# Prompt attention of a hybrid encoder layer: heads taken in pairs, values as the stationary operand, the division by the row sums on GpSimd

## The chip, the cores and the metric

One Trainium2 chip, one of its NeuronCores. The kernel is one program with a queue for each engine: TensorE (matmul and transposes; the profile shows its weight loads apart, as PEld), VectorE (DVE), ScalarE (ACT), GpSimd (POOL) and SyncE (SP, which here only issues DMA transfers). Engines wait for each other on counting semaphores. The metric is the device time of one execution in microseconds.

## The reference, cut to what matters

One layer of an encoder over two groups of rows: a prompt of 1024 tokens and 8 sample sequences of 16. Each layer is a token mixer (latent attention with 8 heads, next to a short gated convolution), a cross attention over 256 memory tokens, and a mixture of 32 experts; a layer norm follows each. The change lies in the prompt group's latent attention:

```python
q = (cq @ w_uq).reshape(B, S, 8, 64 + 32)            # 32 of them rotated (rope)
kn, v = split((lat @ w_ukv).reshape(B, S, 8, 64 + 64))
s = (qn . kn + qr . kr) * (96 ** -0.5)               # kr is shared by the heads
s = where(key_chunk <= query_chunk, s, -inf)         # chunks of 64 tokens
attn = softmax(s) @ v                                # (B, S, 8 * 64)
out = concatenate([attn, y_conv], -1) @ w_out        # 1024 x 1024
```

All data are float32. Products that need full accuracy at the faster rate are made of a rounded high part and the rest, in three products: high x high, high x low, low x high.

## The kernel before

The work runs in stages on the same engines: memory keys and values, the input projection of nine row tiles of 128, then the prompt attention (303 to 472 us from the span's start), the sample group's attention, the output product with its layer norm, cross attention, the experts (over a third of the span), and the last norm.

**The loop over steps.** The attention has 64 steps g, head by head (h = g // 8), each with one tile of 128 queries, in the order 2, 4, 6, 7, 5, 3, 1, 0. Tile i sees (i + 1) x 128 keys. Each engine's queue is written out by hand:

- TensorE: `transposes` (L731) turns the probabilities of step g, up to 8 blocks, into PSUM M0. `scores` (L874) for step g + 2 go into T0 or T1 by turns: three products for each 512 keys. `weigh_values` (L892) for step g - 1 has the turned probabilities of a key block as the stationary operand and 64 value columns as the moving one, in plain float32, each product recorded twice. Between them, in steps 4 to 6, stand `keys` (L868) and `turn_queries` (L861) for the next head.
- VectorE: the copy of the turned probabilities from M0 to SBUF (`prT`, two buffers), the reciprocal of the row sum, `row_max` (L1959) for step g + 2, `scale_rows` (L1964), which multiplies the weighed values of step g - 1 by the reciprocal, and the low parts of keys and queries.
- ScalarE: exp with the row sum as its second output (L1554, `pr`, two buffers), the high parts of keys and queries.
- GpSimd: nothing in the loop.

```python
for g in range(PT * H):
    ...
    transposes(M[0], pr[n % 2], ORDER[n] + 1).then_inc(pT_ps, 1)
    ...
    scores(g + 2)
    ...
    weigh_values(g - 1)
```

Keys and queries of a head lie in one of two sets in SBUF (`kT_hi`, `kT_lo`, `qT_hi`, `qT_lo`). Rows 64 to 95 of the keys are the shared rope part and 8 further rows are the mask; they are filled once for each set, by ScalarE, VectorE and GpSimd.

**Before the loop** TensorE makes the values of all heads in T0, T1, M0 and M1, ScalarE copies them out (L1529), and the first head's keys and queries are made. SP issues in order: two constants, the head loads 1 and 2 from DRAM (`load_head`, L524), the eight parts of `w_out`, the sample group's queries, its cache (2 MB), then a head load each time a buffer is free.

**The output product** takes the attention rows (`attn`, query rows in the partitions) and the convolution rows of a tile, turns both with 8 transposes (`turn_mix`, L1026), splits them (ScalarE L1601, VectorE L1845) and runs 48 products of 512 columns (`three_products`, L1014). GpSimd makes the convolution.

## Time and profile before

| | |
|---|---|
| median of 3 executions | 1645.26 us (1645.1 to 1647.88) |
| the profiled execution: time, span | 1648.83 us, 1647.0 us |
| TensorE busy, its mean granted clock | 1571.5 us (95%), 0.98 |
| VectorE, ScalarE, GpSimd busy | 1018.3, 783.7 and 261.3 us |
| bytes moved, mean rate | 351.72 MB, 214 GB/s |

The span is the time between the first and the last recorded instruction. The time of the execution has 1.83 us around it. Matmul records overlap: each lasts some 0.27 us even where the next starts 0.11 us later, so the time of a run of like matmuls is read from its length less the last record's overhang, not from the mean of one record.

### The profile page before, as it was taken

What the parts mean: (1) busy time and instruction counts of PE and PEld (TensorE: products, weight loads), DVE (VectorE), ACT (ScalarE), POOL (GpSimd) and SP (SyncE); (2) the same over time, 40 slices, a digit from 0 to 9 for tenths busy, and PEclk for the clock granted to TensorE, in tenths of its full rate; (3) what the DMA queues carried; (4) which work ended last, traced back from release to release, by engine and by line L of the source; (5) the groups of instructions that cost most, each with busy time, mean ns of one, the idle gap of its engine ahead of it and who ended that gap; (6) DMA issues with size and microseconds to landing.
All of it is one profiled execution on the core that took longest, in us unless ns stands there. A gap on an engine that the chain in (4) does not pass through costs nothing.

```text
span 1647.0 us, 21343 instructions
## 1 busy us (share of the span) xinstructions
PE 1571.5 (95%) x8472; PEld 1314.8 (80%) x8472; DVE 1018.3 (62%) x1336; ACT 783.7 (48%) x1105; POOL 261.3 (16%) x219
## 2 busy tenths in 40 slices
PE   8999999899998999999999988999999999999956
PEld 6877887788876888999877767888888888888842
DVE  5611111677755556222544548999989989999936
ACT  4411021544445012222422223888888888888824
POOL 0000000300035571000122211111111111111005
PEclk9999999999999999999999987999999999999988
DMA  9721111700021545100345445999999999999877
GB/s 350 257 75 39 41 56 59 250 20 20 3 89 60 226 136 216 66 26 14 128 149 177 161 166 189 378 388 394 384 404 387 393 392 394 387 396 392 322 268 290
DMA packets 85989, 351.72 MB, mean 214 GB/s; under 512 B 23410, under 2 KB 28146, under 8 KB 64132
## 3 DMA queue, kind: packets, MB, share of 16 engines
q1 hardware_dynamic: 75764, 330.43, 53.0%
q0 software_dynamic: 9216, 18.89, 3.0%
q8 instruction: 67, 1.10, 0.3%
q10 hardware_dynamic: 912, 1.05, 0.3%
q14 instruction: 30, 0.25, 0.0%
HBM read 321.93 MB, written 43.15 MB: 222 GB/s over the span
## 4 chain that ended last, share of the span: by engine, by line
PE 90%; DVE 3%; ACT 3%; DMA 2%; issue 1%; POOL 0%; SPq 0%; DVEq 0%; POOLq 0%; ACTq 0%
PE M L1302 26%; PE M L1019 11%; PE T L822 6%; PE M L795 6%; PE T L1302 5%; PE M L899 4%; PE T L731 3%; PE T L1363 2%; PE M L731 2%; PE T L1093 2%; PE T L1091 2%; PE T L1092 2%; PE M L1125 2%; PE M L1107 2%; PE T L1421 2%; DVE rounded L1845 1%
## 5 line engine op out<-in xcount | busy, mean ns | idle before, releaser
L1845 DVE TENSOR_TENSOR rounded<-beside,rounded 128x1024 fp32r<-128x1024 f32 (+1 forms) x397 | 472.9, 1236 | 55.1 <-ACT rounded L1731 41.2
L1302 PE MATMUL M<-rounded 128*128 128x512 f32 x1908 | 461.2, 392 | 2.8 <-ACT rounded L1766 1.9
L1302 PEld LDWEIGHTS M<-rounded 128*128 128x128 f32 x1908 | 355.9, 188 | 77.3 <-ACT rounded L1766 2.1
L1731 ACT CAST rounded<-beside 128x1024 fp32r<-128x1024 f32 x256 | 260.0, 1050 | 72.1 <-DMA beside<-in_w_exp_up 59.6
L1019 PE MATMUL M<-rounded 128*128 128x512 f32 x816 | 196.6, 395 | 2.8 <-ACT rounded L1601 1.6
L1019 PEld LDWEIGHTS M<-rounded 128*128 128x128 f32 x816 | 150.1, 188 | 33.7 <-issue 2.0
L1741 ACT CAST rounded<-beside 128x1024 fp32r<-128x1024 f32 x128 | 128.4, 1051 | 24.8 <-DMA beside<-in_w_exp_down 15.7
L1845 DVE TENSOR_TENSOR rounded<-T,rounded 128x512 fp32r<-128x512 f32 (+2 forms) x98 | 92.6, 948 | 36.8 <-ACT rounded L1614 17.6
L1302 PE MATMUL T<-rounded 128*128 128x512 f32 x384 | 108.7, 398 | 0.0
L2504 POOL DMA_INDIRECT expert_rows<-beside,route_out x32 | 38.9, 1217 | 345.1 <-ACT beside L1772 328.5
L731 PEld LDWEIGHTS T<-tables,arena 128*128 128x128 f32 x548 | 64.3, 143 | 27.7 <-issue 8.8
L731 PE MATMUL T<-tables,arena 128*128 128x128 f32 x548 | 75.2, 280 | 10.0 <-DVE arena L2035 5.3
L1302 PEld LDWEIGHTS T<-rounded 128*128 128x128 f32 x384 | 70.0, 189 | 13.0
L1554 ACT ACTIVATE arena<-T,negmax 128x384 f32<-128x384 f32 (+3 forms) x64 | 47.4, 740 | 68.7 <-DVE negmax L1962 68.7
L2497 POOL DMA_INDIRECT beside<-x_rows,route_tok x32 | 47.6, 1488 | 167.0 <-PE T L1363 149.2
L899 PEld LDWEIGHTS M<-arena 128*128 128x128 f32 x576 | 72.0, 191 | 2.6
L899 PE MATMUL M<-arena 128*128 128x64 f32 x576 | 71.8, 270 | 0.0
L1091 PE MATMUL T<-rounded 128*128 128x256 f32 x248 | 71.0, 286 | 0.0
L1093 PE MATMUL T<-rounded 128*128 128x256 f32 x248 | 70.2, 283 | 0.0
L1092 PE MATMUL T<-rounded 128*128 128x256 f32 x248 | 70.2, 283 | 0.0
L822 PE MATMUL T<-rounded,x_high 128*128 128x512 f32 x270 | 65.4, 394 | 0.0
L795 PE MATMUL M<-rounded,x_high 128*128 128x416 f32 (+1 forms) x270 | 60.6, 375 | 1.1 <-ACT x_high L1447 1.1
(365 smaller groups left out, 2436.1 us busy)
## 6 DMA issues: line engine op xcount, KB each, us to landing
beside<-in_w_exp_gate SPq DMA_DIRECT2D x64, 1024.0 KB, 7.6
beside<-in_w_exp_up SPq DMA_DIRECT2D x64, 1024.0 KB, 10.3
beside<-in_w_exp_down SPq DMA_DIRECT2D x32, 2048.0 KB, 11.3
arena<-x_rows SPq DMA_DIRECT2D x27, 512.0 KB, 4.9
x_rows<-arena SPq DMA_DIRECT2D x18, 512.0 KB, 3.8
arena<-expert_rows SPq DMA_DIRECT2D x9, 1024.0 KB, 13.3
arena<-in_x_prompt SPq DMA_DIRECT2D x16, 512.0 KB, 3.9
arena<-in_cache_mem_k SPq DMA_DIRECT2D x8, 1024.0 KB, 5.6
```

What stands on the lines that cost most here:

```text
L731: got = nc.tensor.transpose(out[:, k * P:(k + 1) * P] if width == P else out[0:width, k * P:(k + 1) * P], rows[:, k * width:(k + 1) * widt ...
L795: got = nc.tensor.matmul(M[u][:, at:at + c1 - c0], x[:, k * P:(k + 1) * P], part[k][:, c0:c1], start=(n_k == 0 and part is w_in_high and x ...
L822: got = nc.tensor.matmul(T[u][:, c:c + CW], x[:, k * P:(k + 1) * P], part[k][:, GC + c:GC + c + CW], start=(k == 0 and part is w_in_high a ...
L899: got = nc.tensor.matmul(o, prT[n % 2][:, c, :], value[:, c, h * DV:(h + 1) * DV], start=(c == 0), stop=(c == i))
L1019: got = nc.tensor.matmul(out[:, c:c + 512], x[k], part(k)[:, c:c + 512], start=(k == 0 and x is hi and part is high), stop=(k == KT - 1 an ...
L1091: nc.tensor.matmul(out, high(k)[:, d * P:(d + 1) * P], x1T[:, 0, k], start=(k == 0), stop=False)
L1092: nc.tensor.matmul(out, high(k)[:, d * P:(d + 1) * P], x1T[:, 1, k], start=False, stop=False)
L1093: got = nc.tensor.matmul(out, low(k)[:, d * P:(d + 1) * P], x1T[:, 0, k], start=False, stop=(k == KT - 1))
L1302: got = nc.tensor.matmul(out, x[xs], (high, low)[ws](w)[:, c:c + 512], start=(first and n == 0), stop=(last and n == 2))
L1731: nc.scalar.copy(as_both(high(c)), both_raw(c)).then_inc(gu_high, 1)
L1741: nc.scalar.copy(high(8 + c), down_raw[:, c, :]).then_inc(down_high, 1)
L1845: return nc.vector.tensor_tensor(out, x, highs.bitcast(f32), ALU.subtract)
```

## The change

- **Pairs.** Steps now go pair by pair: 16 steps for heads 2p and 2p + 1, each query tile for the one head and then for the other. There are four sets of keys and queries (`own_set`). The parts of the next pair (`part_of`, 8 for a pair) are made one a step in steps 2 to 9 of a pair, all in one PSUM bank (`prep_bank`); the first pair's eight parts, in eight banks, ahead of the loop.
- **Values stationary.** `weigh_values(m)` takes both heads of a pair at once: for each key block and each head, 64 value columns are the stationary operand, the turned probabilities (128 queries) the moving one, and the result lands in partitions 0 to 63 or 64 to 127 of M1. ScalarE (`keep_context`) copies it to `attnT`, which is thus turned already. `turn_mix` has only the convolution's four transposes left, and the splits of the output product work on two halves.
- **Division first.** `invert_sum` (VectorE) makes the reciprocal, and GpSimd multiplies the probabilities in place before they are turned. `scale_rows` goes.
- **The lag.** TensorE turns the probabilities of step g - 1 (`turn_probs`), not of step g, and weighs a pair two tiles back; `pr` and `prT` have three buffers.
- **Fills and loads.** The rope and mask rows of three sets are copied from the first by nine small transfers. The `w_out` parts are loaded once 48 steps have their scores. Two of the four value copies go from ScalarE to VectorE.

The diff, cut to its core (removed functions stand above; keys and scores change only in their sets, banks and waits):

```diff
+        with nc.sbuf_tensor("skipped", [P, 26880], f32), nc.sbuf_tensor("attn_turned", [P, 4, 1024], f32) as turned:
+            attnT = turned[:, :, :]
...
-        attn = area(KEEP + 2304, PT, H * DV)
...
-        pr, prT = pair(WORK + 4096, D), pair(WORK + 6144, PT, P)
-        kT_hi, kT_lo, qT_hi, qT_lo = ([rounded[:, at + u * D:at + (u + 1) * D] for u in (0, 1)] for at in (0, 2 * D, 4 * D, 6 * D))
+        pr, prT = pair(WORK + 4096, D) + [area(33536, D)], pair(WORK + 6144, PT, P) + [area(LOWS + D, PT, P)]
+        kT_hi, kT_lo, qT_hi, qT_lo = ([rounded[:, (4 * u + q) * D:(4 * u + q + 1) * D] for u in range(4)] for q in range(4))
...
+        def own_set(h):
+            return 2 * ((h // 2 + 1) % 2) + h % 2
+        def part_of(j):
+            pair_of_heads, r = divmod(j, 8)
+            return 2 * pair_of_heads + r // 2 % 2, r // 4
...
+        PREP_BANKS = [x[:, c:c + 512] for x in (*T, *M) for c in (0, 512)]
+        def prep_bank(j):
+            return PREP_BANKS[min(j, 7)]
+        def prep_in_step(g):
+            k = g % (2 * PT)
+            return 8 * (g // (2 * PT)) + 8 + k - 2 if 2 <= k < 10 and g < 6 * PT else None
...
+        def head_and_tile(g):
+            return 2 * (g // (2 * PT)) + g % 2, ORDER[g // 2 % PT]
...
+            load_head(1, qh[1])
+            sp.wait_ge(head_in[0], 16)
+            load_head(2, qh[0])
+            sp.wait_ge(pads_ready, 2)
+            sp.wait_ge(att_high, 4)
+            sp.wait_ge(kT_ready, 4)
+            for h in (1, 2, 3):
+                for parts, r0, r1 in ((kT_hi, DN, SEEN), (kT_lo, DN, HW), (qT_hi, HW, SEEN)):
+                    sp.dma_start(parts[own_set(h)][r0:r1, :].bitcast(f32), parts[own_set(0)][r0:r1, :].bitcast(f32)).then_inc(sets_in, 16)
...
-            load_head(1, qh[1])
-            sp.wait_ge(head_in[0], 16)
-            load_head(2, qh[0])
-            sp.wait_ge(win_lo_in, 16)
...
-            for k in range(KT):
-                sp.dma_start(w_out_raw[k], w_out_rows[:, k, :]).then_inc(win_lo_in, 16)
             sp.dma_start(q_s, q_dram[PT * P:, :].rearrange("p (h c) -> p h c", h=H)).then_inc(sq_in, 16)
...
-                sp.wait_ge(kT_ps, 2 * (h - 2) + 2)
+                sp.wait_ge(qT_ps, 4 * ((h - 2) // 2) + 3 + h % 2)
                 load_head(h, qh[h % 2])
-            sp.wait_ge(kT_ps, 2 * H)
+            sp.wait_ge(s_ps, 3 * 2 * PT)
+            for k in range(KT):
+                sp.dma_start(w_out_raw[k], w_out_rows[:, k, :]).then_inc(win_lo_in, 16)
+            sp.wait_ge(qT_ps, 2 * H)
...
-            sp.wait_ge(o_done, 2 + PT * H)
+            sp.wait_ge(o_done, 2 + PT * H // 2)
...
-            sp.wait_ge(rowsT_ps, PT)
+            sp.wait_ge(rows_low, PT)
...
+            def turn_queries(j):
+                h, half = part_of(j)
+                if j > 7:
+                    pe.wait_ge(kT_ready, 4 + j // 2 + 1)
+                pe.wait_ge(head_in[h % 2], 16 * (h // 2) + 16)
+                q = qh[h % 2] if h else q_first
+                for i in range(4):
+                    got = nc.tensor.transpose(prep_bank(j)[0:HW, i * P:(i + 1) * P], q[:, 4 * half + i, :], ident)
+                got.then_inc(qT_ps, 1)
...
+            def turn_probs(g):
+                pe.wait_ge(rrms_ready, NT + g + 1)
+                pe.wait_ge(pT_ready, g + 1)
+                transposes(M[0], pr[g % 3], head_and_tile(g)[1] + 1).then_inc(pT_ps, 1)
+            def weigh_values(m):
+                h, i = head_and_tile(2 * m)
+                pe.wait_ge(pT_ready, 2 * m + 3)
+                pe.wait_ge(o_done, m + 2)
                 for c in range(i + 1):
-                    got = nc.tensor.matmul(o, prT[n % 2][:, c, :], value[:, c, h * DV:(h + 1) * DV], start=(c == 0), stop=(c == i))
+                    for s in (0, 1):
+                        got = nc.tensor.matmul(M[1][s * DV:(s + 1) * DV, m % 2 * P:(m % 2 + 1) * P], value[:, c, (h + s) * DV:(h + s + 1) * DV],
+                                               prT[(2 * m + s) % 3][:, c, :], start=(c == 0), stop=(c == i))
                 got.then_inc(o_ps, 1)
...
-                h, n = divmod(g, PT)
-                pe.wait_ge(exp_done, g + 3)
-                pe.wait_ge(pT_ready, g + 1)
-                transposes(M[0], pr[n % 2], ORDER[n] + 1).then_inc(pT_ps, 1)
-                if n == 6 and h + 1 < H:
-                    pe.wait_ge(kT_ready, 4 + 2 * (h + 1) + 1)
-                    keys(h + 1, 1)
                 if g + 2 < PT * H:
                     scores(g + 2)
-                if n == 4 and h + 1 < H:
-                    pe.wait_ge(head_in[(h + 1) % 2], 16 * ((h + 1) // 2) + 16)
-                    keys(h + 1, 0)
-                if n == 5 and h + 1 < H:
-                    turn_queries(h + 1, 0)
-                    turn_queries(h + 1, 1)
+                j = prep_in_step(g)
+                if j is not None:
+                    (turn_queries if j % 2 else keys)(j)
+                if g % 2 == 0 and g > 2:
+                    weigh_values(g // 2 - 2)
                 if g > 0:
-                    weigh_values(g - 1)
-            weigh_values(PT * H - 1)
+                    turn_probs(g - 1)
+            weigh_values(PT * H // 2 - 2)
+            turn_probs(PT * H - 1)
+            weigh_values(PT * H // 2 - 1)
...
-                if t < PT:
-                    transposes(T[u], attn[:, t, :], 4)
                 transposes(T[u][:, 512:], conv_rows[t % 4], 4).then_inc(rowsT_ps, 1)
...
-            for c, src in enumerate((T[0], T[1], M[0], M[1])):
+            for c, src in enumerate((T[0], T[1])):
                 act.wait_ge(value_ps, c + 1)
...
-            keys_high(0, 1)
+            def part_high(j):
+                (h, half), cols = part_of(j), slice(part_of(j)[1] * 512, part_of(j)[1] * 512 + 512)
+                if j % 2:
+                    act.wait_ge(qT_ps, j // 2 + 1)
+                    nc.scalar.mul(qT_hi[own_set(h)][0:HW, cols], prep_bank(j)[0:HW, :], MLA_SCALE).then_inc(att_high, 1)
+                else:
+                    act.wait_ge(kT_ps, j // 2 + 1)
+                    nc.scalar.copy(kT_hi[own_set(h)][0:DN, cols], prep_bank(j)[0:DN, :]).then_inc(att_high, 1)
+            def exponentials(g):
+                w = (head_and_tile(g)[1] + 1) * P
+                act.wait_ge(negmax_ready, g + 1)
+                if g > 2:
+                    act.wait_ge(pT_ps, g - 2)
+                nc.scalar.activation(pr[g % 3][:, 0:w], T[g % 2][:, 0:w], ACT.Exp, bias=negmax[g % 2][:, 0:1],
+                                     scale=1.0, accum_out=rsum[g % 2][:, 0:1]).then_inc(exp_done, 1)
+            def keep_context(m):
+                h, i = head_and_tile(2 * m)
+                act.wait_ge(o_ps, m + 1)
+                nc.scalar.copy(attnT[:, h // 2, i * P:(i + 1) * P], M[1][:, m % 2 * P:(m % 2 + 1) * P]).then_inc(o_done, 1)
+            for j in range(6):
+                part_high(j)
+            exponentials(0)
+            part_high(6)
+            part_high(7)
...
+                if g + 1 < PT * H:
+                    exponentials(g + 1)
+                if prep_in_step(g) is not None:
+                    part_high(prep_in_step(g))
+                if g % 2 == 0 and g > 2:
+                    keep_context(g // 2 - 2)
+            keep_context(PT * H // 2 - 2)
+            keep_context(PT * H // 2 - 1)
...
-                act.wait_ge(rowsT_ps, t + 1)
...
                 if t < PT:
-                    nc.scalar.copy(rows_hi[u], T[u][:, :]).then_inc(rows_high, 1)
+                    act.wait_ge(o_done, 2 + PT * H // 2)
+                    nc.scalar.copy(rows_hi[u][:, 0:512].rearrange("p (k c) -> p k c", k=4), attnT[:, :, t * P:(t + 1) * P])
+                act.wait_ge(rowsT_ps, t + 1)
+                if t < PT:
+                    nc.scalar.copy(rows_hi[u][:, 512:], T[u][:, 512:]).then_inc(rows_high, 1)
...
+            for c, src in enumerate(M):
+                dve.wait_ge(value_ps, c + 3)
+                nc.vector.tensor_copy(value[:, 2 * c + 4:2 * c + 6, :].rearrange("p i c -> p (i c)"), src[:, :]).then_inc(q_turned, 1)
...
-            def scale_rows(g):
-                h, n = divmod(g, PT)
-                s = g % 2
-                dve.wait_ge(o_ps, g + 1)
...
+                nc.vector.tensor_reduce(negmax[g % 2][:, 0:1], T[g % 2][:, 0:(head_and_tile(g)[1] + 1) * P], AX.X, ALU.max, negate=True).then_inc(negmax_ready, 1)
+            def invert_sum(g):
+                dve.wait_ge(exp_done, 2 + g + 1)
+                if g > 1:
+                    dve.wait_ge(rrms_ready, NT + g - 1)
+                nc.vector.reciprocal(rinv[g % 2][:, 0:1], rsum[g % 2][:, 0:1]).then_inc(norm_done, 1)
+            def keep_turned(g):
+                dve.wait_ge(pT_ps, g + 1)
+                if g > 2:
+                    dve.wait_ge(o_ps, (g - 3) // 2 + 1)
+                i = head_and_tile(g)[1]
+                nc.vector.tensor_copy(prT[g % 3][:, 0:i + 1, :].rearrange("p i c -> p (i c)"), M[0][:, 0:(i + 1) * P]).then_inc(pT_ready, 1)
+            for j in range(4):
...
+                invert_sum(g)
+                if g > 1:
+                    keep_turned(g - 2)
                 if g + 2 < PT * H:
                     row_max(g + 2)
...
+                if prep_in_step(g) is not None:
+                    part_low(prep_in_step(g))
+            keep_turned(PT * H - 2)
+            keep_turned(PT * H - 1)
...
-                    take_low(rows_lo[u], T[u][:, :], rows_hi[u]).then_inc(rows_low, 1)
+                    take_low(rows_lo[u][:, 0:512].rearrange("p (k c) -> p k c", k=4), attnT[:, :, t * P:(t + 1) * P],
+                             rows_hi[u][:, 0:512].rearrange("p (k c) -> p k c", k=4))
+                    take_low(rows_lo[u][:, 512:], T[u][:, 512:], rows_hi[u][:, 512:]).then_inc(rows_low, 1)
...
+            for g in range(PT * H):
+                w = (head_and_tile(g)[1] + 1) * P
+                pool.wait_ge(norm_done, NT + g + 1)
+                if g == PT * H - 4:
+                    pool.wait_ge(qT_ps, 2 * H)
+                    pool.wait_ge(kT_ps, 2 * H)
+                    nc.gpsimd.memset(kr_all[:, 0:DN], 0.0)
+                    for u in (0, 1):
+                        got = nc.gpsimd.memset(krTb[u][0:DN, :], 0.0)
+                    got.then_inc(pads_ready, 1)
+                nc.gpsimd.tensor_scalar(pr[g % 3][:, 0:w], pr[g % 3][:, 0:w], rinv[g % 2][:, 0:1], None, ALU.mult).then_inc(rrms_ready, 1)
+            pool.sem_inc(pads_ready, 1)
```

## Rows read from the trace of the kernel before

**Rows 1.** The page: TensorE's busy time (share of the span), and the chain that ended last.
```profile
PE 1571.5 (95%) x8472; PEld 1314.8 (80%) x8472; DVE 1018.3 (62%) x1336; ACT 783.7 (48%) x1105; POOL 261.3 (16%) x219
...
PE 90%; DVE 3%; ACT 3%; DMA 2%; issue 1%; POOL 0%; SPq 0%; DVEq 0%; POOLq 0%; ACTq 0%
```

**Rows 2.** Windows, one head: PE, PEld, DVE, ACT, POOL busy, PEclk, DMA share, GB/s.
```profile
366.55:387.80 21.25, 20.71 (x158) 19.12 (x158) 16.22 (x37) 8.66 (x21) 0.00 (x0) 1.00 0.08 19
```

**Rows 3.** The chain in order of time: start, duration, records of L899.
```profile
315.05 1.51 PE M L899 x14
...
463.92 1.51 PE M L899 x14
```

**Rows 4.** Timeline of one head, TensorE: start, duration, line, operands.
```profile
380.78 0.36 PE L887 MATMUL T<-rounded 104*128 104x256 f32 x1
...
381.09 0.28 PE L889 MATMUL T<-rounded 96*128 96x256 f32 x1
...
381.21 0.39 PE L870 MATMUL T<-rounded,x_low 128*64 128x512 f32 x1
...
381.67 0.39 PE L872 MATMUL T<-rounded,x_low 128*64 128x512 f32 x1
...
381.89 1.89 PE L899 MATMUL M<-arena 128*128 128x64 f32 x16
...
383.99 0.31 PE L887 MATMUL T<-rounded 104*128 104x128 f32 x1
...
384.35 0.61 PE L865 MATMUL T<-tables,arena 128*96 128x128 f32 x4
```

**Rows 5.** Timeline of the output stage, TensorE, one tile and the next.
```profile
556.60 1.03 PE L731 MATMUL T<-tables,arena 128*128 128x128 f32 x8
...
557.39 11.15 PE L1019 MATMUL M<-rounded 128*128 128x512 f32 x48
...
568.38 1.04 PE L731 MATMUL T<-tables,arena 128*128 128x128 f32 x8
```

**Rows 6.** Timeline, the end of the sample group's attention, TensorE.
```profile
526.46 1.16 PE L986 MATMUL M<-arena 128*128 128x128 f32 x8 [0.82 <-ACT arena L1572]
...
528.41 1.09 PE L1009 MATMUL T<-beside 128*64 128x128 f32 x16 [0.38 <-DVE beside L2002]
```

**Rows 7.** Lines by form, one head: count, busy us, mean ns, idle before.
```profile
L1968 DVE TENSOR_SCALAR arena<-M,rinv 128x64 f32<-128x64 f32 x8 | 2.2, 281 | 2.8 <-PE M L899 2.8
...
L1980 DVE COPY arena<-M 128x1024 f32<-128x1024 f32 x1 | 1.2, 1225 | 0.5 <-PE M L731 0.5
...
L1980 DVE COPY arena<-M 128x768 f32<-128x768 f32 x1 | 1.0, 958 | 0.3 <-PE M L731 0.3
...
L1980 DVE COPY arena<-M 128x512 f32<-128x512 f32 x1 | 0.7, 692 | 0.1
```

**Rows 8.** Lines by form, GpSimd, the whole execution.
```profile
L2539 POOL TENSOR_TENSOR arena<-arena 128x1024 f32<-128x1024 f32 x7 | 16.5, 2363 | 4.4 <-ACT arena L1826 4.4
...
L2426 POOL TENSOR_SCALAR rounded<-tables 8x512 fp32r<-8x512 f32 x4 | 7.5, 1874 | 0.3
...
L2430 POOL CAST rounded<-beside 32x1024 fp32r<-32x1024 f32 x1 | 1.0, 1032 | 0.2 <-POOL rounded L2426 0.2
```

**Rows 9.** Timeline of the attention's start, four engines.
```profile
295.68 2.47 POOL L2426 TENSOR_SCALAR rounded<-tables 8x512 fp32r<-8x512 f32 x1
...
302.36 0.44 PE L870 MATMUL T<-rounded,x_low 128*64 128x512 f32 x1 [1.45 <-DVE rounded L1845]
...
303.16 0.42 PE L887 MATMUL T<-rounded 104*128 104x384 f32 x1
...
304.73 0.47 PE L887 MATMUL T<-rounded 104*128 104x512 f32 x1 [0.81 <-DVE rounded L1845]
...
309.75 0.43 SPq L550 DMA_DIRECT2D arena<-in_cache_kv_latent  x1
```

**Rows 10.** The tile q_rows: its transfers, from issue to landing.
```profile
DMA to landing us min/median/max: 2.3/3.1/11.6
```

More of the change, by code:

```diff
@@ L1976, in _ @@
+            part_low(7)
             for g in range(PT * H):
[L1977 to L1985 removed]
+                invert_sum(g)
+                if g > 1:
+                    keep_turned(g - 2)
```

162 lines of the change are left out of this document (54 added, 108 removed).

## The prediction

> **What bounds the kernel now.** I read the page first: the span of 1647.0 us lies inside a profiled execution of 1648.83, which is 3.57 above the median of 1645.26. TensorE is busy for 95% of the span and holds 90% of the chain that ended last [rows 1]. So a change pays by what it takes off TensorE's stream, or costs by the waits that it puts into it.
>
> The change touches the prompt attention, the stretch from 303 to 472. The windows show what that stretch is made of: one head takes 21.25 us, of which TensorE is busy 20.7, VectorE 16.2, ScalarE 8.7 and GpSimd 0, at a granted clock of 1.00, the upper level (2.4 GHz) [rows 2]. The chain shows the same period seven times: the block of 14 value records that starts at 315.05 starts again at 463.92, 148.87 later, 21.27 a head [rows 3]. Nearly all of the period is TensorE's own issue. Four rows of it give unit prices. Sixteen value records (8 products, two records each) last 1.89; with the last record's 0.27 taken off, that is 0.108 from one to the next. Eight transposes in 1.04 make 0.11 each [rows 4, 5]. A 512-column product takes 0.23 (two from 381.21 to 381.67) [rows 4]. I write W for a tile's width in blocks of 128 keys; a head has W = 1 to 8, 36 blocks. Then a head costs 36 x 0.22 = 7.9 for weighing, 36 x 0.11 = 4.0 for turning probabilities, and 6 x 0.23 + 8 x 0.11 = 2.3 for keys and queries; the remaining 7.1 of the 21.27 are scores.
>
> **Weighing the values.** Before, the probabilities are stationary (128 columns) and 64 value columns move. After, 64 value columns are stationary, 128 probability columns move, and the two heads of a pair write partitions 0 to 63 and 64 to 127 in turn. The number of records stays: 2 x 36 x 8 = 576. Their spacing is the question. The kernel already has one place with the new shape: line 1009, stationary 128x64, moving 128x128, outputs in the lower and upper 64 partitions in turn. Its 16 records last 1.09, so (1.09 - 0.27)/15 = 0.055 each; line 986, the same moving size with 128 stationary columns, needs (1.16 - 0.27)/7 = 0.127 [rows 6]. Bounds: 0.055 (both halves run at once) and 0.110 (they don't). I take 0.055, the row with the same shapes and the same order. That takes 576 x (0.110 - 0.055) = 31.7 off TensorE, 3.96 a head.
>
> The Trainium skill's TensorEngine Tiling page (Key Properties) speaks against this: changing the tiling mode, not just the tile, drains the array. There are 32 weighing blocks, so 64 changes. The trace disagrees where keys (line 870, 128x64 stationary) stand between full-width instructions: the 256-column product at 381.09 is followed at 381.21, and the value block follows the last 512-column keys product by 0.22, the usual spacings [rows 4]. So the sum has nothing for it; it is a rival below.
>
> **VectorE and ScalarE.** Scaling the output (L1968) goes: 8 x 0.28 [rows 7]; neighbours overlap by some 0.06 (a head's listed durations add up to 18.2, its window to 16.2), so 8 x 0.22 = 1.8 is saved and 14.4 a head is left. Row maxima, copies, reciprocals and the low parts stay. ScalarE gains four copies of 128x128 a head, some 0.3 each, for 9.9. Both stay under TensorE's 21.3 - 4.0 = 17.3. Neither is the bound by its total.
>
> **GpSimd** gets the division: 4608 columns a head, in place, of which the trace shows no example. Nearest rows: a cast, one input, 1.03 for 1024 columns; a two-input product 2.36 for 1024; a tensor_scalar over 8 partitions and an odd layout 1.87 for 512 [rows 8]. That is 1.0, 2.3 and 3.7 ns a column, or 4.7, 10.6 and 16.9 us a head. I take 2.3, the dense 128-partition row; both ends lie below 17.3. The lag of one step is what hides it: the division of the even step 6 (W = 8) starts about 1 us into TensorE's step 6, and its transposes are issued 5.3 after that step's start. So up to some 4 us are covered, and 2.4 are needed.
>
> **Waits that come in.** Now step k of a pair is scores(k+2), a key or query part in k = 2 to 9, weighing in even k, then turning k-1. Turning writes M0, which is one buffer, so it waits until the previous copy has left M0: 0.16 of pipeline, 0.15 of hand-over and the copy itself. In even steps the weighing lies in front and covers it. Odd steps have only scores (and a query part, 0.44) in front. Scores take 0.75 for W = 4, 0.43 for W = 2 (380.78 to 381.21) and 0.36 for W = 1 (383.99 to 384.35) [rows 4]; copies take 1.23, 0.96 and 0.69 for W = 8, 6 and 4 [rows 7], and by the same slope 0.42 for W = 2. Step 9: 1.55 - (0.75 + 0.44) = 0.35. Step 11: 1.28 - 0.43 = 0.85. Step 13: 1.00 - 0.36 = 0.65. Step 15: 0.74 - 0.59 = 0.15. Add 0.3 at the turn of a pair, where exp of the next pair stands behind ScalarE's context copy. That is 2.3 for each of three pairs. The last pair has no key and query parts as cover: 0.25 more in step 7 and 0.45 more in step 9, 3.0. Together 9.9. Steps 4 to 8 should have none: their step pairs cost TensorE 6.1 against VectorE's 5.3. What is late behind a waiting turning is the next step's scores, then the maximum. Bounds: 0 and twice this, 20.
>
> **The start.** All eight parts of heads 0 and 1 now stand ahead of scores(0). Two value copies move to VectorE (1.2 each), so the four end at about 300.3 and not at 301.1. The parts go into eight different banks and cost 2 x 2.3 = 4.6 from 298.9, against two waits before (1.45 and 0.81) [rows 9]. So scores(0) comes at 303.4 against 303.16. Scores(1) needs the nine small transfers that fill the other sets. SP issues them behind two head loads, at 0.43 each from about 298.2 (it waits for the GpSimd masks and VectorE's low rope rows, both done by 296.8), and the last lands near 304.5; before, scores(1) ran at 304.73. I take 0. Head 1's queries are now needed at 300.7 rather than a head later: load_head landings are 2.3 to 11.6, median 3.1 [rows 10], from an issue at 297.3 in front of, not behind, the two constants. 3.2 is hidden; at 7.2 it would cost 4, at 11.6 it would cost 8. Head 3's load stands behind 2 MB of cache rows (issued at 309.75 before [rows 9], about 305 after); it would have to be in at about 318.8, and I expect 316. The weights of the output product (4 MB, 8.24 of issue) move to step 46. They are first read some 40 us after that, so they cost nothing; without that cover it would be 12. The 0 to 8 goes into the range.
>
> **The output stage.** turn_mix loses four of eight transposes in each of eight tiles: 8 x 4 x 0.10 = 3.2, all on TensorE, which stands in an unbroken row of transposes and 48 products [rows 5]. At its start the copy and subtraction work on halves, the first of which is there already: about 0.8. ScalarE's and VectorE's extra fixed costs lie in a stage where they idle. 4.0 in all; bounds 3 and 5.
>
> **Sum.** 31.7 - 9.9 - 0 + 4.0 = 25.8 off. Against its own time 1648.83 becomes 1623.0; against the median 1645.26 it becomes 1619.5. I forecast 1619.
>
> **Rivals.**
> - *The halves don't run at once* (0.110 per record): 31.7 comes back while the waits stay (their cover is not in the weighing). 1619 + 32 = 1651, slower. It decides when the spacing is above some 0.10. Line 1009's row is against it. Chance 3%.
> - *GpSimd is the bound.* It has 36,864 columns. At 3.7 ns a column the steps that turn W = 7 to 6 need 19.7 against TensorE's 17.8, 2 a pair: 1627. To be slower than before it needs over (169 + 4)/36,864 = 4.7 ns; one of the four tensor_scalar rows comes to 2.47 for 512, 4.8, while VectorE ran [rows 9]: 1651. Chances 5% and 3%. For it: no row of the real shape. Against it: both dense rows.
> - *A drain at each change of tile shape.* 64 times what a record shows beyond its spacing, 0.27 - 0.055 = 0.2: 13 more, 1632. The rows at 381.09 to 381.89 are against it; the page on tiling named above is for it. Chance 4%.
> - *Handing over costs more*: five engines now pass one probability tile on, and VectorE at 14.4 of 17.3 has little slack. If each of 64 steps loses a further 0.2, it is 13: 1632, with the upper bound of the waits 1629. For it: VectorE's queue is in order, so a maximum stands behind a copy that stands behind TensorE. Chance 14%.
> - The forecast itself: 71%, with a range of its own of 1609 (no waits in odd steps) to 1627 (a start late by 8).
>
> **How the numbers follow.** 0.2% is 3.3 us, about what a measurement of this kernel can tell from no change. Slower: the two 3% cases, less a little, 5%. Same: between them and the others, 2%. Faster: 93%. The range takes in the forecast's own, the drain, the 3.7 ns and most of the hand-over case: 1608 to 1633.
>
> **What would show it.** L899's successor: 16 records in about 1.1, not 1.9. The period of a pair: 37 instead of 42.5; TensorE busy about 34 of it; waits of some 0.3 to 0.9 ahead of the turning in the narrow tiles, released by VectorE's copy. GpSimd's tensor_scalar over 1024 columns: at or below 2.4. Scores(0) at 303 to 304. Tiles of the output stage 11.4 apart, not 11.8. The prediction is wrong if the spacing stays at 0.11, if the turning waits on GpSimd, or if the middle steps (W = 6 to 8), not the narrow ones, hold the waits.

## The result and the profile after

The changed kernel takes 1632.35 us, the kernel before 1646.57 on the same chip (medians of four runs each): a ratio of 0.9918 with a 95% interval of 0.9903 to 0.9934. A second comparison (a0 below) gave 0.9934 (0.9921 to 0.9948). So 11 to 14 us are gained where 25.8 were forecast. The profiled execution took 1636.98 with a span of 1634.5.

The page's busy times, engine by engine (share of the span, count of instructions), to be read against [rows 1]:

```profile
PE 1552.7 (95%) x8440; PEld 1282.0 (78%) x8440; DVE 1005.3 (62%) x1282; ACT 786.8 (48%) x1143; POOL 362.7 (22%) x277
```

TensorE is still the bound, so what counts is its stream. I cut it into stages at instructions that both kernels have.

| stage | before | after | saved | forecast |
|---|---|---|---|---|
| attention, from scores(0) to the first instruction behind its last weighing | 169.06 | 161.46 | 7.6 | 21.8 |
| sample group, up to the output stage | 56.19 | 54.20 | 2.0 | 0 |
| output stage, start and tiles | 112.45 | 109.12 | 3.3 | 4.0 |

The 2.0 of the sample group nobody had forecast, and the change didn't earn it. The windows of this stage before, after, and in a0, which is the changed kernel once more (PEclk is TensorE's mean granted clock, 1.00 the upper level):

```profile
core 0: us, PE busy (x) PEld busy (x) DVE busy (x) ACT busy (x) POOL busy (x), PEclk, DMA share, GB/s
472.22:528.41 56.19, 49.29 (x282) 34.78 (x281) 28.97 (x43) 30.46 (x58) 36.54 (x27) 0.97 0.22 76
465.87:520.07 54.20, 47.63 (x283) 34.21 (x281) 28.09 (x41) 30.81 (x59) 36.22 (x24) 1.00 0.23 78
463.69:519.77 56.08, 49.32 (x283) 34.80 (x281) 28.25 (x41) 30.69 (x59) 35.46 (x24) 0.97 0.23 76
```

The changed kernel itself takes 56.08 here at a mean granted clock of 0.97 and 54.20 at 1.00; e2 and e7, which edit nothing in this stage, take 54.16 and 54.34 at 1.00. So of the profiled saving only the 7.6 and the 3.3, 10.9 in all, belong to the change. The shortfall is all in the attention: 14.2 us. Two stretches of it, first the steady state. The window is one period of a pair long, from a place in one pair to the same place in the next, with the same columns:

```profile
352.10:390.60 38.50, 36.78 (x318) 29.91 (x317) 28.97 (x56) 20.00 (x48) 27.53 (x16) 1.00 0.09 21
```

A pair of heads takes 38.50 at the upper clock, where two heads took 2 x 21.25 [rows 2] and 37.0 was forecast. The timeline of TensorE (start, length, records of one run of like instructions, the wait in brackets) shows steps 8 to 13 of a pair:

```profile
413.17 0.39 PE L896 MATMUL M<-rounded,x_low 128*64 128x512 f32 x1
413.40 0.40 PE L897 MATMUL M<-rounded,x_low 128*64 128x512 f32 x1
413.73 1.75 PE L937 MATMUL M<-arena 128*64 128x128 f32 x28
415.41 1.09 PE L760 MATMUL M<-tables,arena 128*128 128x128 f32 x8
416.25 0.48 PE L921 MATMUL T<-rounded 104*128 104x512 f32 x1
...
417.91 0.84 PE L760 MATMUL M<-tables,arena 128*128 128x128 f32 x6 [0.28 <-DVE arena L2027]
...
422.95 0.63 PE L760 MATMUL M<-tables,arena 128*128 128x128 f32 x4 [0.79 <-DVE arena L2027]
...
426.79 0.41 PE L760 MATMUL M<-tables,arena 128*128 128x128 f32 x2 [0.59 <-DVE arena L2027]
```

Read it from the starts. Twenty-eight weighing records last 1.75, so (1.75 - 0.27)/27 = 0.055 each: the forecast spacing. The waits for VectorE's copy stand in the odd steps 9, 11 and 13 and nowhere else: 0.28, 0.79, 0.59. What nobody had priced is at the block's edges. The last keys product starts at 413.40 and the weighing at 413.73, 0.33 later; before, that distance was 0.22 [rows 4]. And 28 x 0.055 = 1.54 after 413.73 the transposes could have begun; they begin at 415.41, 0.14 late. The weight loads say the same:

```profile
413.18 0.13 PEld L897 LDWEIGHTS M<-rounded,x_low 128*64 128x64 f32 x1
413.72 1.51 PEld L937 LDWEIGHTS M<-arena 128*64 128x64 f32 x28 [0.41 <-issue]
415.40 0.64 PEld L760 LDWEIGHTS M<-tables,arena 128*128 128x128 f32 x6 [0.17 <-POOL arena L2493]
```

The load for L897 is made 0.22 before its product; those of the first weighing record and of the first transpose only 0.01 before.

The second stretch is the start. TensorE's and SP's timelines and the chain:

```profile
304.41 0.42 PE L921 MATMUL T<-rounded 104*128 104x384 f32 x1
...
311.24 0.66 PE L921 MATMUL T<-rounded 104*128 104x384 f32 x1 [6.05 <-DMA rounded<-rounded]
```

```profile
298.03 1.02 SPq L547 DMA_DIRECT2D arena<-q_rows  x2
299.17 7.46 SPq L570 DMA_DIRECT2D rounded<-rounded  x9
```

```profile
305.86 5.25 DMA rounded<-rounded
```

Scores(1) waits 6.05 for the nine fills. They take 7.46 to issue, 0.83 each and not the 0.43 that the sum had, and the last lands 5.25 after 305.86. The first products behind the wait last 0.66 and 0.63 where the same forms take 0.42 and 0.48 later: the granted clock of the stretch from 304.41 to 342.10 is 0.86, so a part of it ran at the lower level, 1.2 GHz, after TensorE had stood idle (0.51 in the 8.06 us from 311.24 on). Scores(0) themselves stand at 304.41, where 303 to 304 was said. But the value products ahead of them already begin 1.1 later than before (294.36 against 293.25; in a0 it is 291.81), behind stages that the change doesn't touch; from there to scores(0) it is 10.05 against 9.91.

GpSimd's division is a row that the trace before lacked (total, mean ns):

```profile
L2493 POOL TENSOR_SCALAR arena<-arena,rinv 128x1024 f32<-128x1024 f32 x8 | 22.7, 2844 | 2.7 <-DVE rinv L2020 2.7
L2493 POOL TENSOR_SCALAR arena<-arena,rinv 128x128 f32<-128x128 f32 x8 | 4.8, 603 | 8.2 <-DVE rinv L2020 8.2
```

That is (2844 - 603)/896 = 2.5 ns a column and 0.28 fixed. The output stage:

```profile
536.04 11.18 PE L1054 MATMUL M<-rounded 128*128 128x512 f32 x48
547.06 0.60 PE L760 MATMUL T<-tables,arena 128*128 128x128 f32 x4
547.41 11.16 PE L1054 MATMUL M<-rounded 128*128 128x512 f32 x48
```

Tiles are 11.37 apart instead of 11.78 [rows 5], with four transposes ahead of each.

### The profile page after: what moved, and what is told of

The parts are those of the page before. It is cut to its first block, busy times and chain, and to the rows that moved or that the text cites. A ratio compares the mean times of both kernels' runs of the same rounds, so it can differ in the third digit from the quotient of the medians.

```text
span 1634.5 us, 21436 instructions
## 1 busy us (share of the span) xinstructions
PE 1552.7 (95%) x8440; PEld 1282.0 (78%) x8440; DVE 1005.3 (62%) x1282; ACT 786.8 (48%) x1143; POOL 362.7 (22%) x277
## 4 chain that ended last, share of the span: by engine, by line
PE 89%; DVE 4%; ACT 3%; DMA 2%; issue 1%; SPq 1%; POOL 0%; DVEq 0%; POOLq 0%; ACTq 0%
PE M L1335 26%; PE M L1054 11%; PE T L851 6%; PE M L824 6%; PE T L1335 5%; PE T L760 3%; PE M L760 3%; PE T L1396 3%; PE M L937 2%; PE T L1126 2%; PE T L1124 2%; PE T L1125 2%; PE M L1158 2%; PE M L1140 2%; PE T L1454 2%; DVE rounded L1892 1%
## 5 line engine op out<-in xcount | busy, mean ns | idle before, releaser
L1778 ACT CAST rounded<-beside 128x1024 fp32r<-128x1024 f32 x256 | 258.8, 1049 | 78.8 <-DMA beside<-in_w_exp_up 72.8
L1788 ACT CAST rounded<-beside 128x1024 fp32r<-128x1024 f32 x128 | 125.0, 1048 | 27.2 <-DMA beside<-in_w_exp_down 26.7
L2493 POOL TENSOR_SCALAR arena<-arena,rinv 128x384 f32<-128x384 f32 (+7 forms) x64 | 110.0, 1724 | 57.0 <-DVE rinv L2020 56.8
L1892 DVE TENSOR_TENSOR rounded<-T,rounded 128x512 fp32r<-128x512 f32 (+2 forms) x84 | 79.1, 944 | 19.3 <-ACT rounded L1661 17.7
L760 PEld LDWEIGHTS T<-tables,arena 128*128 128x128 f32 x516 | 60.5, 143 | 26.8 <-issue 8.2
L760 PE MATMUL T<-tables,arena 128*128 128x128 f32 x516 | 71.4, 280 | 10.3 <-DVE arena L2087 5.5
L2553 POOL DMA_INDIRECT beside<-x_rows,route_tok x32 | 43.8, 1370 | 118.0 <-PE T L1396 100.8
L1578 ACT ACTIVATE arena<-T,negmax 128x384 f32<-128x384 f32 (+7 forms) x64 | 47.4, 741 | 44.5 <-PE M L760 26.4
L2027 DVE COPY arena<-M 128x384 f32<-128x384 f32 (+7 forms) x64 | 48.0, 749 | 28.2 <-PE M L760 27.8
## 6 DMA issues: line engine op xcount, KB each, us to landing
arena<-expert_rows SPq DMA_DIRECT2D x9, 1024.0 KB, 12.8
```

Of the source, the lines that this page charges most:

```text
L760: got = nc.tensor.transpose(out[:, k * P:(k + 1) * P] if width == P else out[0:width, k * P:(k + 1) * P], rows[:, k * width:(k + 1) * widt ...
L1778: nc.scalar.copy(as_both(high(c)), both_raw(c)).then_inc(gu_high, 1)
L1788: nc.scalar.copy(high(8 + c), down_raw[:, c, :]).then_inc(down_high, 1)
L1892: return nc.vector.tensor_tensor(out, x, highs.bitcast(f32), ALU.subtract)
L2493: nc.gpsimd.tensor_scalar(pr[g % 3][:, 0:w], pr[g % 3][:, 0:w], rinv[g % 2][:, 0:1], None, ALU.mult).then_inc(rrms_ready, 1)
```

## Experiments

Two questions: what are the 7 us at the start, and what holds a pair 1.5 above forecast. Each comparison below is with the changed kernel; "stage" is the time from scores(0) to the first instruction behind the last weighing, 161.9 in a0 (301.83 to 463.7). The stage and the pair carry the argument, not the totals: the runs are spread over chips on which the kernel before took 1645.66 to 1650.26, and stages that no run edits move with the clock, as seen above. Between the profiled executions of the changed kernel and of e7, which turns out to change nothing in it, the stage varies by 0.8 (161.1 to 161.9).

**a0, nothing edited.**

> The changed kernel once more, nothing edited, beside the next three on one chip. Every theory: within 3 us of 1632, scores(1) 6 us late behind the last of the nine fills, a pair of heads in 38.5.

1634.19 us (1632.29 to 1636.13); the wait ahead of scores(1) 5.7, a pair 38.50. This is the yardstick for e5, e7 and e8, which ran on its chip.

**e1, the fills counted apart.**

```diff
- ....then_inc(sets_in, 16)
+ ....then_inc(zeros_ready if h == 1 else sets_in, 16)
...
  if g == 1:
-     pe.wait_ge(sets_in, 16 + 3 * 48)
+     pe.wait_ge(zeros_ready, 1 + 48)
+ if g == 2 * PT:
+     pe.wait_ge(sets_in, 16 + 2 * 48)
```

> The kernel after the change, with the nine fills of the three other sets counted apart: scores(1) waits only for the three fills of head 1's set, the first scores of the second pair (step 16) wait for the other six. In the changed kernel the nine took 7.46 us to issue (299.17 to 306.6), the last landed 5.25 later and TensorE stood 6.3 us ahead of scores(1). If the start was lost to issuing nine of them behind one another, head 1's three are issued in 2.5 and land some 2 to 5 later: 4 to 6 us less than the changed kernel, and the wait ahead of scores(1) at most 2. Rival: each small transfer is late of itself behind the head loads and the 2 MB of cache rows, or the loop's next wait takes the place of this one (head 3's load, the maxima); then under 2 us less.

Ratio to before 0.9886 (0.9869 to 0.9902), on the chip where the kernel before was slowest (1650.26); the stage fell only from 161.9 to 159.4, 2.4 where 4 to 6 were expected. Scores(1) now start at once, 0.82 after scores(0), and the next wait takes the place, as the rival had it:

```profile
302.15 0.42 PE L923 MATMUL T<-rounded 104*128 104x384 f32 x1
...
302.97 0.42 PE L923 MATMUL T<-rounded 104*128 104x384 f32 x1
...
321.72 0.61 PE L906 MATMUL M<-tables,arena 128*96 128x128 f32 x4 [3.65 <-DMA arena<-q_rows]
322.17 1.34 PE L760 MATMUL M<-tables,arena 128*128 128x128 f32 x7
```

Head 3's queries are asked for at 311.17, behind the 2 MB of cache rows (asked for at 307.12), and TensorE waits for them until 321.72. Seven transposes then last 1.34 where they take 0.98 at the upper clock.

**e8, head 3's load ahead of the cache rows, on top of e1.**

```diff
  # behind the nine fills
+ sp.wait_ge(qT_ps, 4)
+ load_head(3, qh[1])
  sp.dma_start(shift2, ...)
...
- for h in range(3, H):
+ for h in range(4, H):
```

> The kernel with the fills counted apart, and the load of head 3 issued right behind the nine fills, ahead of the constants and the 2 MB of cache rows. There TensorE stood 3.65 us at 321.7 for that load and went on at the lower clock. If the two waits are one loss that only moves (fills first, head 3 next), both go now: scores(1) at once, no wait for head 3, 4 to 5 us less than with the fills alone, 9 to 11 less than the changed kernel. Rival: the fills and three head loads share the queue, and head 3 lands no earlier than 321, or the next load (head 4) becomes late: within 2 us of the fills alone.

1628.04 (1625.14 to 1631.49), 6.15 below a0; ratio to before 0.9897 (0.9881 to 0.9914). The stage takes 154.0, 7.8 less. From scores(0) to the 32-record weighing of the first pair it is 302.78 to 332.94, 30.2, where the changed kernel needed 304.41 to 342.10, 37.7. So the start had cost 7.5, idle time and lower clock together (the granted clock of this stretch is 1.00 in e8, 0.86 in the changed kernel). What TensorE still waits for in the window from 295 to 465 (total, times, longest; left out are one wait behind the attention and 1.2 in two waits for VectorE's low parts):

```profile
PE M L762 <- DVE arena L2031: 7.9, 14, 0.8
...
PE T L925 <- DMA rounded<-rounded: 0.4, 1, 0.4
PE M L941 <- DVE arena L2031: 0.4, 1, 0.4
```

The nine fills still take 7.57 to issue; TensorE now waits 0.4 for those of head 1, and for the others not at all. The 9 to 11 that I expected were too high, for the total and for the stage.

**e3, the old operands in the new schedule.** The output has the context in another layout, so that the product behind it reads other values.

```diff
- for c in range(i + 1):
-     for s in (0, 1):
-         got = nc.tensor.matmul(M[1][s * DV:(s + 1) * DV, m % 2 * P:(m % 2 + 1) * P], value[...], prT[...][:, c, :], ...)
+ for s in (0, 1):
+     for c in range(i + 1):
+         got = nc.tensor.matmul(M[1][:, m % 2 * P + s * DV:m % 2 * P + (s + 1) * DV], prT[...][:, c, :], value[...], ...)
```

> The kernel after the change with the old operands of the weighing alone: turned probabilities stationary (128 columns), 64 value columns moving, 128x64 outputs. The order of steps, the division on GpSimd, the pairs and the lag stay; the context lands in another layout, so the output product reads other values in the same time. If the new operands are worth the 0.055 us a record for which they were forecast, 576 records cost 31.7 more; if changes of tile shape cost about 0.1 each in the changed kernel, 64 of them come back, 6.4: 25 us slower than the changed kernel. With changes of shape free: 32 slower. If the gain was not in the spacing: within 5.

1661.84 (one run; before 1650.26 on that chip). Its span of 1659.6 is 25.1 above that of the changed kernel, close to the 25 expected, but that is luck: its sample group, which isn't edited, takes 60.1 at a lower clock where the changed kernel's took 54.2. The stage is 183.4, 21.5 above a0, the pair 44.0. Its timeline at the same place as above:

```profile
422.72 0.40 PE L897 MATMUL M<-rounded,x_low 128*64 128x512 f32 x1
422.95 3.24 PE L937 MATMUL M<-arena 128*128 128x64 f32 x28
426.02 1.05 PE L760 MATMUL M<-tables,arena 128*128 128x128 f32 x8
426.82 0.47 PE L921 MATMUL T<-rounded 104*128 104x512 f32 x1
```

Both edges are gone: 0.23 on entering, and 28 x 0.110 = 3.07 from the block's start to the transposes. The transposes, too, take 0.80 to the next scores instead of 0.84. So a weighing with the new operands pays 0.10 + 0.14 + 0.04 = 0.28 at its edges, 9.0 for 32 blocks. Counted by pairs it is the same: 144 records at 0.055 less are worth 7.9, the pair is only 5.5 shorter (44.0 to 38.5), 2.4 is paid back, 0.30 a block. The waits have no part in it: e3's pair has the same three, 1.6 in all, and so have the pairs of e4, e10 and e5 below. The edges are dearer than the 6.4 for which the expectation had them.

**e4 and e10, do the halves run at once?** e4 exchanges the two loops, so that one head's blocks come in a row, then the other's. e10 does that and also puts both heads into partitions 0 to 63, with a copy for each:

```diff
+ got = nc.tensor.matmul(M[1][0:DV, (m % 2 + 2 * s) * P:(m % 2 + 2 * s + 1) * P], value[...], prT[...], ...)
...
+ for s in (0, 1):
+     got = nc.scalar.copy(attnT[s * DV:(s + 1) * DV, h // 2, i * P:(i + 1) * P], M[1][0:DV, (m % 2 + 2 * s) * P:...])
```

> The kernel after the change with the weighing's two loops exchanged: all key blocks of the one head (lower half of the outputs), then all of the other (upper half). Same records, same operands. If the spacing of 0.055 comes from two neighbours in different halves running at once, a record now takes about 0.11 and the kernel is 25 to 32 us slower than the changed one. If 0.055 is what 128 moving columns take anyway: within 2 us.

> The kernel of one head after the other, with both heads' results in partitions 0 to 63 of M1 (four column blocks), so that TensorE's upper output half is never used and ScalarE copies each head's part by itself. Still 64-column stationaries, 128 columns moving, some 0.10 a record. The kernel of one head after the other took a pair of heads in 43.4. If the delay on entering and leaving a weighing comes from any 64-column stationary beside full ones, it stays, and the pair stays at 43.4. If it comes with the use of the upper half (the keys products, lower half only, show no delay among full-width neighbours), it goes: 8 x 0.24, so 41.5 a pair, 7 to 8 us less than the 1654 of one head after the other. ScalarE's extra copy, some 0.25 in every second step, lies beside TensorE.

e4 took 1654.09, a pair 43.37; e10 took 1666.45, a pair 46.64 (one run each). TensorE's timeline, e4:

```profile
422.29 2.89 PE L937 MATMUL M<-arena 128*64 128x128 f32 x28
```

and e10:

```profile
430.06 0.40 PE L897 MATMUL M<-rounded,x_low 128*64 128x512 f32 x1
430.38 3.27 PE L937 MATMUL M<-arena 128*64 128x128 f32 x28
433.59 1.09 PE L760 MATMUL M<-tables,arena 128*128 128x128 f32 x8
```

In one half alone a record takes (3.27 - 0.27)/27 = 0.111, and the pair is 46.64 - 38.50 = 8.1 longer than the changed kernel's, 144 x 0.056. The forecast's bounds, 0.055 and 0.110, were right, and the gain is the two halves running at once. e4's 18 to 21 us (by the spans) are below the 25 to 32 expected: where it goes over from one half to the other they overlap too, 0.4 a block. In e10 that overlap is gone, which neither of its two expected pairs, 43.4 and 41.5, had counted. My theory of e10 fell: the edges didn't go with the upper half. Entering still takes 0.32, and the transposes follow 3.21 after a start, 0.10 above 28 x 0.111.

**e5, more edges.**

```diff
  for g in range(PT * H):
+     if g % 2 == 0 and g > 2:
+         weigh_values(g // 2 - 2, part=0)      # key block 0 alone
      ...scores, keys or queries...
-         weigh_values(g // 2 - 2)
+         weigh_values(g // 2 - 2, part=1)      # the others
```

> The changed kernel, with the first key block of each weighing (4 records) moved ahead of the step's scores, the rest where it was: same records, 28 more stretches of half-width stationaries between full-width instructions, and no wait ahead of the second part. In the changed kernel a weighing starts 0.10 later and is followed 0.14 later than spacing alone makes it (0.33 and 0.20 on entering instead of 0.23 and 0.12; with the old operands both delays were gone). If it is the change between half-array and full-array instructions that costs, 28 more of each cost 6.7 us, 1.7 in each pair of heads. If the delay belongs to the waits ahead of a weighing (turned probabilities, free output), it isn't paid twice: within 1 us.

1642.17 (one run), 8.0 above a0; the stage 170.2 (302.4 to 472.6), 8.3 longer; a pair 40.94. Seven blocks of a pair are split, so an additional stretch costs 2.44/7 = 0.35, more than the 0.24 expected because these stand behind transposes:

```profile
421.46 0.85 PE L760 MATMUL M<-tables,arena 128*128 128x128 f32 x6 [0.26 <-DVE arena L2033]
422.24 0.44 PE L940 MATMUL M<-arena 128*64 128x128 f32 x4
422.61 0.39 PE L921 MATMUL T<-rounded 104*128 104x256 f32 x1
```

Six transposes reach to the next instruction in 0.78 where scores follow them in 0.60, and four records (0.22) in 0.37. The second part, ahead of which no semaphore is waited for, starts at 423.16, 0.20 behind the last scores (422.96), which follow each other by 0.12 to 0.13. The edge is paid each time, with or without a semaphore near it.

**e13, between which instructions does it lie?**

```diff
- nc.tensor.matmul(out, wk_lo[:, head], latT_hi[:, rows], start=False, stop=True)
+ nc.tensor.matmul(out, wk_lo[:, head].bitcast(f32), latT_hi[:, rows].bitcast(f32), start=False, stop=True)
```

> The changed kernel, with the last of the three keys products in plain float32 (the other two as they were, on rounded parts). It has the same 64-column stationary and a 512-column moving operand, and stands right ahead of the weighing, whose products are plain float32 too. In the changed kernel the weighing starts 0.33 after the last keys product where 0.23 is the spacing. If the delay of 0.10 lies between rounded and plain products with a 64-column stationary, it moves ahead of the plain keys product (0.33 after the rounded one instead of 0.23), and the weighing follows at spacing. If the delay belongs to the weighing itself, whatever stands ahead, the plain keys product starts 0.23 after the rounded one and the weighing is still 0.10 late. In either case 24 products in the loop become slower (512 columns at the plain rate, of which the trace has only 128-column examples at 0.055 to 0.127 a record): by 4 times that, two records each, some 0.4 to 1.0 us more a product, 10 to 24 us in all.

```profile
409.59 0.39 PE L895 MATMUL M<-rounded,x_low 128*64 128x512 f32 x1
409.82 0.40 PE L896 MATMUL M<-rounded,x_low 128*64 128x512 f32 x1
410.14 0.64 PE L897 MATMUL M<-rounded,x_low 128*64 128x512 f32 x1
410.16 0.43 PE L937 MATMUL M<-arena 128*64 128x128 f32 x2
410.62 0.59 PE L897 MATMUL M<-rounded,x_low 128*64 128x512 f32 x1
```

The delay moved: from the second keys product to the third, now plain, it is 0.32 instead of 0.23, and two weighing records start 0.02 behind it and end before its second record starts. So two products with the same 64-column stationary differ. The reading that fits e3, e5 and this run is that the plain float32 ones use half the array, side by side with the other half, while the rounded ones take the whole array, and that the edge lies between the two ways. The last part is inferred: no run puts rounded products into the two halves by turns, and a record doesn't name its half. The Trainium skill's TensorEngine Tiling page (Key Properties) has this rule: changing the tiling mode drains the engine. By it, and by e3, e5 and e13, each of the 32 weighings pays on entering and on leaving. The time, 1640.89 (one run), is not the 10 to 24 above the changed kernel that I expected, and the miss is one of counting: the loop makes 12 parts of keys with one such product each, not 24, so the price of 0.4 to 1.0 a product came to 5 to 12. The pair takes 40.97, 2.5 more for four such products, 0.62 each.

**e7, the division cut to 128 columns** (the other columns stay undivided).

> The changed kernel, with the division on GpSimd cut to the first 128 columns of each tile (0.6 us a step, 38.6 in all instead of 110; the other columns stay undivided). If the handing over through GpSimd holds nothing, as the forecast had it (2.8 us for the widest tile, covered by the lag of one step), the period of a pair stays 38.5 and the time within 1 us. If the division is part of what is late, each of the even steps around the widest tiles gives back up to 0.2 and the pair falls by 1 us or more: 3 to 5 us in all.

1633.88 (one run) against 1634.19. GpSimd is busy 9.69 of a pair's 38.51 instead of 27.53, and the pair is as long as before:

```profile
341.04:379.55 38.51, 36.80 (x319) 29.91 (x320) 28.96 (x57) 20.06 (x49) 9.69 (x16) 1.00 0.09 22
```

In the steady state the division is wholly covered.

**e2, e9, e11, the waits for the copy.** e2 turns narrow tiles (up to 4 blocks) into the two banks of M0 by turns. e9 is e8 with e2. e11 is e9 with the copy of a wide tile cut in two, each half released by itself:

```diff
- pe.wait_ge(pT_ready, g + 1)
- transposes(M[0], pr[g % 3], ...)
+ # e2: narrow behind narrow waits one step less, in the other bank
+ pe.wait_ge(pT_ready, g if g > 0 and narrow(g) and narrow(g - 1) else g + 1)
+ transposes(M[0][:, 512 * (g % 2) if narrow(g) else 0:], pr[g % 3], ...)
```

> The kernel after the change, with the probabilities of narrow tiles (up to 4 blocks) turned into the two halves of M0 by turns, so that the turning doesn't wait for VectorE's copy of the step before. In the changed kernel TensorE waits for that copy 0.28, 0.79, 0.59 and less in the odd steps 9, 11, 13 of a pair. If that wait is the 9.9 us of waits in the forecast, it gives back 1.3 to 1.9 us a pair, 5 to 7.5 in all. Rival: the turning then waits for the division (GpSimd was busy 27.5 of the 38.5 us of a pair) or for the exponential instead, since the chain of one tile is as long as before: under 2 us less.

> The two mended loads (fills counted apart, head 3 ahead of the cache rows) and the narrow tiles in two banks by turns. Alone the loads gave 6 us against the changed kernel on the same chip, the banks took 0.4 off each pair of heads (38.5 to 38.1). If the two losses are apart from each other: 1.6 below the loads alone, 7.5 to 8 below the changed kernel. If the turning that no longer waits for VectorE's copy now waits for GpSimd because the start no longer is late: no lower than the loads alone.

> The two mended loads, the narrow tiles by turns in the two banks of M0, and the copies of wide tiles cut in two, so that the turning of the next tile's first four blocks waits for the first bank alone. Of 7.9 us of waits for VectorE's copy (14 in the stage), the 0.28, 0.79 and 0.59 of each pair then go. If they are a loss of their own, the pair falls from 38.5 to 37.0 or a little under, 5 to 6 us below the loads alone. Rival: VectorE pays for the second copy (40 more, some 0.1 each, in a queue that the maxima share) and the chain exponential, reciprocal, division, turning, copy is as long as before, so the wait moves to the division or the exponential: 2 us or less.

e2: ratio to before 0.9885 (0.9869 to 0.9902), but the pair fell only to 38.10 and the stage to 158.8, 3.0 below a0 where 5 to 7.5 were expected. Of the three waits the 0.59 alone goes; those of steps 9 and 11 stand behind a wide tile's copy, which holds both banks, as I should have seen before. Exp then holds scores for 0.19. e9: 1626.94 (1623.87 to 1627.7), ratio 0.9890 (0.9873 to 0.9906), the stage 152.0, the pair 38.13. e11: 1625.04 (lowest 1620.99; a single one of its four executions took 5446, which I can't explain), ratio 0.9865 (0.9843 to 0.9888), the stage 149.0 (302.94 to 451.97):

```profile
332.69:370.12 37.43, 36.66 (x319) 29.90 (x320) 29.28 (x65) 20.03 (x49) 27.57 (x16) 1.00 0.09 23
```

So the pair lost 1.07 of the 1.5 expected, and the last wait for the copy in the middle is 0.52, with 0.18 for exp beside it; the stage is 5.0 below e8, where 5 to 6 were expected. This is the best version: 12.8 less in the stage than a0, though in the whole time the intervals of e8, e9 and e11 overlap.

## Why the prediction was right in its mechanism and too high in its gain

It said faster, within 1608 to 1633, by three terms. Their sum was 25.8, measured are 11 to 14, of which the profiles give 10.9 to the attention and the output stage. Two terms that the sum had at nothing failed. That 1632 still lies in the range is luck: its upper part stood for a late head 1, a slow division, costly handing over or the drain, each alone, and what filled it was the drain's cost together with a late start of another cause. Point by point:

- *The bound and the mechanism* hold. The spacing is 0.055; e10 shows the other bound, 0.111. Rival one is refuted.
- *"So the sum has nothing for it", of the change of tile shape,* is the first step that failed. It cost 0.28 a weighing, 9 us in all (e3; e5 gives 0.35 at another place), of the 13 of that rival, to which I gave 4%. The rule that I set aside there is the one that the runs bear out. My evidence was the keys products in [rows 4]. They have the same 64-column stationary but are rounded, and in e13 the edge stands between them and the plain ones. The row had the right shape and the wrong type. So 31.7 came out as 21.5 (e3 against a0).
- *"I take 0", of the start,* is the second: 7.5 us (e8 against the changed kernel, from scores(0) to the same weighing). I took 0.43 for the issue of a fill from single large loads; measured are 0.83, and a landing of 5.25. I had put a late start into the range with another cause, head 1's queries, and had expected head 3's at 316. They were in time only because the fills had already held TensorE; e1 has them at 321.7.
- *The waits, 9.9:* their places are as forecast, odd steps, narrow tiles, VectorE's copy. The sum is 8.3 (7.9 in 14 waits, and 0.4 ahead of a weighing), 1.66 in a steady pair for 2.3: the small ones, of step 15 and at the turn of a pair, are not there. The even steps of the steady pairs are free of waits. TensorE is busy for 36.8 of a pair where "about 34" was said; the edges are the most of that.
- *GpSimd:* 2.84 for 1024 columns, above the "at or below 2.4" that I named as a sign, yet covered (e7). The step was right, its number a fifth too low. Both GpSimd rivals fall.
- *Two rivals at 1632.* Both the drain (4%) and the handing over (14%) had named the time that came. Of the drain the cause is there, at 9 for 13, and without the start it would have left the time 7.5 lower; of the handing over it isn't: no wait of 0.2 a step.
- *The output stage:* 3.3 for 4.0, its start 0.8 and a tile 0.41 shorter as forecast.

The attention's shortfall of 14.2 is then: the start 7.5; four pairs, each taken as 1.5 above forecast, 6.0; 0.7 left, no more than the stage varies without an edit. A pair can be counted from the two heads before, 42.5. Off go 144 records x 0.053 = 7.6, and 1.1 for two waits of 0.56 at head turns that the sum had overlooked; seven of them stood in the attention before:

```profile
PE T L887 <- issue: 3.9, 7, 0.6
```

On top come 1.7 of waits and 2.4 of edges, which makes 37.9. The 0.6 that are left to 38.5 I haven't told apart.

## What to carry to other kernels

Before a product is costed by a row, match its type and its neighbours as well as its shape: two products with stationaries of equal shape behaved differently here, and each block of the one kind cost 0.10 to 0.18 on entering and 0.14 on leaving, so few long blocks of the one kind are worth more than many short ones. Small transfers that one queue issues in a row are costed by their issue and by what is behind them in the same queue; count them apart, and put the load that is needed first ahead of the large one. When a late transfer is mended, look at once for the next that it had hidden. Before a stage's gain is credited to an edit, look at its granted clock: here 2 us of a stage that nobody had touched came and went with it.

## What the runs showed of the hardware

- Plain float32 products with 64-column stationaries in alternating output halves run two at once, 0.055 a record against 0.111 in one half (e10), and 128-column records run beside a 512-column product of the other head's half (e13, 410.16 to 410.59).
- The passage between them and full-width or rounded instructions, in either direction, shows as a weight load that isn't made ahead: 0.01 before its product, not 0.22. It costs 0.10 behind a 512-column product, 0.18 behind transposes (e5), 0.14 on leaving and 0.04 in the transposes behind it.
- A fill of 8 to 40 partitions (32 to 160 KB) from SBUF to SBUF takes 0.83 us to issue in the mean, behind two head loads (nine in 7.46; 7.57 and 7.80 in e8 and e1).
- TensorE's granted clock went to its lower level around the idle time of 6.05 us (0.86 from 304.41 to 342.10) and around e1's of 3.65 (0.95 from 302.15 to 337.64); with neither, in e8, the same stretch has 1.00. The sample group, with nothing edited, has 0.97 in some executions (56.1 us) and 1.00 in others (54.2).
- GpSimd's one-input multiplication by a scalar per partition costs 2.5 ns a column and 0.28 fixed, beside VectorE at 75% busy (2844 ns for 1024 columns, 603 for 128).
